# Attention heads placed between the query blocks of a fused two-block network, with the shifted turn beside the values and the last projection in column parts

## The chip, the cores and the metric

The kernel runs on one NeuronCore of one Trainium2 chip. The metric is the device time of one launch in microseconds, the median over three runs.

TensorE is PE in the profile (its weight loads PEld), ScalarE ACT, VectorE DVE, GpSimd POOL, SyncE SP (it only issues transfers). Each runs its own program in order; they meet at semaphores.

## What is computed

Sequence 256, model width 2048, all in float32. A first block (windowed attention, a recurrent unit, a layer of experts) and a state-space layer come first and stay as they are. The change is in the last layer, a dilated attention whose keys and values come from the unshifted input x of the layer:

```python
k, v = split(x @ kv_w, 2)                 # 3 groups x 8 heads x 128 each
h = x * (1 + scale) + shift               # scale, shift, gate: silu(c) @ ada_w + ada_b
q, z = split(h @ in_w, [3072])            # 3 x 8 x 128 query columns, 1024 for z
...
for g, (window, dilation) in enumerate(DIL_PATTERNS):
    o, lse = _dilated_window_attention(q[:, :, g], k_sh[:, :, g], v_sh[:, :, g],
                                       window, dilation, slopes[g])
...
o = einsum("blghe,blgh->blhe", o, softmax(lse over g)) * silu(z)
y = o @ out_w                             # 1024 x 2048
x = _layer_norm(ALPHA * x + (1.0 + gate) * y, ln_g, ln_b)
```

The three groups of a head share one softmax over all their scores, since the weights of the groups come from their log-sums.

## The kernel before

**Weights.** Every weight matrix is streamed in tiles of 128 x 1024 (512 KB) in the order of the table STREAM, four buffers deep. SyncE loads a tile into raw; ScalarE copies it to w_hi in TensorE's reduced format (L1119, "high part"; it waits until TensorE has done with the tile that had the buffer, four tiles before); VectorE subtracts to get the rest, w_lo (L1580, "low part"). TensorE forms each product as three matmuls: high with high, high with low, low with high. A tile's count goes through the semaphores raw_loaded, hi_done, lo_done and tile_used. FIRST_BODY[name] is the first group of four tiles of a matrix.

**Products.** The transposed input is held as xt_hi and xt_lo, 16 pieces of 128 channels x 256 tokens. In block_product two tiles give one block of 128 output channels (48 matmuls with 256 columns, L528 to L530), and banks 0 and 1 of PSUM alternate. In token_columns a tile gives 12 matmuls of 512 columns (L581 to L583), tokens on the partitions. For a new input, turn transposes X (L625), and ScalarE and VectorE make the 16 pieces (L1156, L1632, L1640).

**Order of the last layer.** k2 (24 blocks), v2 (3 groups of 16 tiles into banks 0 to 3; each is evicted at L1537 before the next), with the ada sums for this layer's scale and gate ahead of the third group; then the turn of the shifted input; q2 (24 blocks, evicted into q2T at L1544); z2 (16 tiles into banks 4 to 7, then Silu at L1551). Then the 8 heads, in a loop of two: GpSimd copies a head's three query pieces to q_st (L516), TensorE forms the scores (L1066, L1069), VectorE adds distances and finds the maxima (L2288 to L2303), ScalarE takes the exponentials (L1557, L1559), TensorE transposes them (L1077), ScalarE copies them out (L1562, L1564), TensorE multiplies with the values (L1082, L1086), and VectorE scales and gates (L2312) in zn. The eight outputs are transposed (L1104), copied to oT, split into high and low, and b_out (16 tiles, L600 to L604) accumulates all 2048 output columns in all 8 banks at once. Last, gate_rows spreads the gate over the partitions by matmuls with a diagonal (built by GpSimd, L490; matmuls L1034), and layer_norm runs over whole rows: product times gate (L2227), residual (L2230), sums and squares on ScalarE (L1517, L1521), root (L1160), and two operations a token half on VectorE (L2240, L2245), each half of the tokens then stored.

The text of each engine's program sets the order.

## Time and profile before

| | us |
|---|---|
| median of 3 runs | 3613.61 (3612.01 to 3614.05) |
| the profiled execution, its own time | 3612.69 |
| its span, first to last instruction | 3611.0 |
| TensorE busy in it | 3369.3 (93%) |
| granted TensorE clock, mean | 0.966 of 2.4 GHz |

The profile is of one execution; its times count from the first instruction, and v2 starts at 3120.6 us. Busy time of an engine says nothing of what it holds up: for that the waits and the chain of work are read. A granted clock (PEclk) of 1.00 is 2.4 GHz, 0.50 is 1.2 GHz.

### The profile page before, as it was taken

The numbers are of one execution on the slowest core, as the hardware profiler recorded it, in microseconds if no ns is written. First come the engines' busy times: TensorE is split into PE (matmuls) and PEld (weight loads), VectorE is DVE, ScalarE is ACT, GpSimd is POOL, SyncE is SP. The second block draws the span as 40 slices with busy tenths as digits, with TensorE's granted clock in tenths as the row PEclk, the third lists the DMA queues.
The fourth block names the chain that finished last, engine by engine and source line by source line (L and its number), as shares of the span: only waits on it lengthen the run. The fifth ranks groups of instructions, "written<-read, shape, count | busy, mean of one in ns | idle before, by whom it ended". The sixth has DMA issues, their size and how long they took to land.

```text
span 3611.0 us, 70869 instructions
## 1 busy us (share of the span) xinstructions
PE 3369.3 (93%) x24282; PEld 3043.7 (84%) x24282; DVE 2245.7 (62%) x3639; ACT 1636.7 (45%) x2226; POOL 679.6 (19%) x620
## 2 busy tenths in 40 slices
PE   7989999999999999999999889999997979999986
PEld 7878999999889988998778679987775859978965
DVE  6674476377777777777777743346554876545454
ACT  4654455433443345333445446653433444334443
POOL 1000049500110011000001148851113111100010
PEclk9999999999999999999999989999997989999998
DMA  6425545666886678666558725554443767755622
GB/s 189 147 82 164 162 143 162 181 203 201 261 262 197 203 240 266 213 203 187 164 159 272 236 83 182 182 164 147 135 141 107 264 211 233 243 177 151 184 78 93
DMA packets 181819, 656.59 MB, mean 182 GB/s; under 512 B 23040, under 2 KB 23184, under 8 KB 180576
## 3 DMA queue, kind: packets, MB, share of 16 engines
q1 hardware_dynamic: 149328, 545.82, 48.9%
q0 software_dynamic: 32400, 109.56, 9.7%
q8 instruction: 57, 0.93, 0.1%
q14 instruction: 34, 0.28, 0.0%
HBM read 653.18 MB, written 2.10 MB: 181 GB/s over the span
## 4 chain that ended last, share of the span: by engine, by line
PE 83%; DVE 5%; issue 4%; ACT 3%; PEld 2%; POOL 2%; DMA 0%; DVEq 0%; ACTq 0%; POOLq 0%; PEldq 0%; SPq 0%
PE PS L528 14%; PE PS L529 13%; PE PS L530 13%; PE PS L857 7%; PE PS L861 6%; PE PS L859 6%; PE PS L810 2%; PE PS L600 2%; PE PS L602 2%; PE PS L604 2%; PE PS L581 2%; PE PS L582 2%; PE PS L583 2%; POOL w_lo L429 2%; PE PS L1011 1%
## 5 line engine op out<-in xcount | busy, mean ns | idle before, releaser
L1119 ACT ACTIVATE w_hi<-raw 128x1024 fp32r<-128x1024 f32 x1032 | 1092.5, 1060 | 1657.0 <-PE PS L530 945.3
L1580 DVE TENSOR_TENSOR w_lo<-raw,w_hi 128x1024 fp32r<-128x1024 f32 x872 | 1070.9, 1230 | 898.2 <-ACT w_hi L1119 893.6
L528 PE MATMUL PS<-xt_hi,w_hi 128*128 128x256 f32 x4608 | 1326.3, 288 | 20.5 <-DVEq L2106 8.5
L529 PE MATMUL PS<-xt_lo,w_hi 128*128 128x256 f32 x4608 | 1309.6, 284 | 0.0
L530 PE MATMUL PS<-xt_hi,w_lo 128*128 128x256 f32 x4608 | 1308.8, 284 | 0.0
L528 PEld LDWEIGHTS PS<-xt_hi,w_hi 128*128 128x128 f32 x4608 | 890.0, 193 | 34.3 <-issue 25.6
L529 PEld LDWEIGHTS PS<-xt_lo,w_hi 128*128 128x128 f32 x4608 | 890.6, 193 | 0.0
L530 PEld LDWEIGHTS PS<-xt_hi,w_lo 128*128 128x128 f32 x4608 | 890.1, 193 | 0.0
L429 POOL TENSOR_TENSOR w_lo<-raw,w_hi 128x1024 fp32r<-128x1024 f32 x160 | 402.3, 2540 | 241.7 <-ACT w_hi L1119 241.3
L857 PE MATMUL PS<-w_hi,st_hi 128*128 128x512 f32 x1024 | 403.0, 394 | 0.2
L859 PE MATMUL PS<-w_hi,st_lo 128*128 128x512 f32 x1024 | 399.8, 390 | 0.0
L861 PE MATMUL PS<-w_lo,st_hi 128*128 128x512 f32 x1024 | 399.5, 390 | 0.0
L443 POOL DMA_DIRECT2D ada<-in_ada_w x240 | 128.9, 537 | 1230.1 <-DVE acc_down L1954 652.2
L857 PEld LDWEIGHTS PS<-w_hi,st_hi 128*128 128x128 f32 x1024 | 193.0, 188 | 40.3 <-ACT hid L1363 1.0
L861 PEld LDWEIGHTS PS<-w_lo,st_hi 128*128 128x128 f32 x1024 | 192.8, 188 | 40.3
L859 PEld LDWEIGHTS PS<-w_hi,st_lo 128*128 128x128 f32 x1024 | 193.0, 189 | 39.1
L581 PE MATMUL PS<-w_hi,xt_hi 128*128 128x512 f32 x352 | 140.8, 400 | 3.6 <-ACT v2n L1537 3.6
L600 PE MATMUL PS<-w_hi,st_hi 128*128 128x512 f32 x320 | 126.6, 396 | 14.8 <-DVE st_lo L1598 14.8
L582 PE MATMUL PS<-w_hi,xt_lo 128*128 128x512 f32 x352 | 138.9, 395 | 0.0
L583 PE MATMUL PS<-w_lo,xt_hi 128*128 128x512 f32 x352 | 138.8, 394 | 0.0
L1928 DVE TENSOR_TENSOR hot<-iota,slotsT 128x256 bf16<-128x256 bf16 (+1 forms) x256 | 113.4, 484 | 29.0 <-PEq L802 29.0
L602 PE MATMUL PS<-w_hi,st_lo 128*128 128x512 f32 x320 | 126.4, 395 | 0.0
(369 smaller groups left out, 3540.4 us busy)
## 6 DMA issues: line engine op xcount, KB each, us to landing
raw<-in_u_emb SPq DMA_DIRECT2D x256, 512.0 KB, 3.8
raw<-in_v_emb SPq DMA_DIRECT2D x256, 512.0 KB, 4.3
ada<-in_ada_w POOLq DMA_DIRECT2D x240, 256.0 KB, 3.7
raw<-in_xbc SPq DMA_DIRECT2D x96, 512.0 KB, 3.9
raw<-in_z SPq DMA_DIRECT2D x80, 512.0 KB, 3.6
raw<-in_q SPq DMA_DIRECT2D x64, 512.0 KB, 3.5
raw<-in_a_out SPq DMA_DIRECT2D x64, 512.0 KB, 4.8
raw<-in_k SPq DMA_DIRECT2D x48, 512.0 KB, 4.2
```

The costliest lines, as they stand in the source:

```text
L429: pool.tensor_tensor(w_lo[:, u, :], raw[:, u, :], w_hi[:, u, :].bitcast(F32), ALU.subtract)\
L528: pe.matmul(o, w_h, x_h, start=start, stop=False, skip_group_check=True)
L529: pe.matmul(o, w_h, x_l, start=False, stop=False, skip_group_check=True)
L530: return pe.matmul(o, w_l, x_h, start=False, stop=stop, skip_group_check=True)
L581: pe.matmul(o, xt_hi[:, k, t], w_hi[:, u, c:c + 512], start=k == 0, stop=False)
L582: pe.matmul(o, xt_lo[:, k, t], w_hi[:, u, c:c + 512], start=False, stop=False)
L583: last = pe.matmul(o, xt_hi[:, k, t], w_lo[:, u, c:c + 512], start=False, stop=k == KC - 1)
L857: pe.matmul(o, st(st_hi, st2_hi, u)[:, t], w_hi[:, u, c], start=start, stop=False, skip_group_check=True)
L859: pe.matmul(o, st(st_lo, st2_lo, u)[:, t], w_hi[:, u, c], start=False, stop=False, skip_group_check=True)
L861: last = pe.matmul(o, st(st_hi, st2_hi, u)[:, t], w_lo[:, u, c], start=False, stop=stop, skip_group_check=True)
L1119: act.activation(w_hi[:, u, :], raw[:, u, :], ACT.Copy).then_inc(hi_done, 1)
L1580: dve.tensor_tensor(w_lo[:, u, :], raw[:, u, :], w_hi[:, u, :].bitcast(F32), ALU.subtract)\
```

## The change

z2 is streamed ahead of q2. The values are made in 6 groups of 8 tiles that alternate between banks 0, 1 and 2, 3. The ada sums and the 16 transposes of the shifted input stand between tiles of the values, and the shifted pieces go to buffers of their own (xt2_hi, xt2_lo, q2T is gone). The columns of q2 are stored head by head, so that blocks 3h to 3h+2 give the queries of head h, which ScalarE evicts straight into q_st; the steps of head h stand between the blocks of head h+1, those of the last head between tiles of b_out. The outputs of each head are transposed and split into o_hi and o_lo at once. b_out is taken in four parts of 512 columns (two banks each), in the order OUT_TILES; the gate row is spread between its tiles, and VectorE adds a part and takes its statistics with BN_STATS while later parts run. The norm is finished by half rows, which are stored in four transfers. The last layer's steps on TensorE, ScalarE and VectorE are written out without loops, except k2 and z2 on the latter two.

```diff
-    ("xbc", 24), ("z", 16), ("a_out", 16), ("k2", 12), ("v2", 12), ("q2", 12), ("z2", 4), ("b_out", 4),
+    ("xbc", 24), ("z", 16), ("a_out", 16), ("k2", 12), ("v2", 12), ("z2", 4), ("q2", 12), ("b_out", 4),
...
+OUT_TILES = [(part, pair) for part in (0, 1) for pair in range(3)] + [(0, 3), (1, 3)] \
+    + [(part, pair) for part in (2, 3) for pair in range(4)]
...
-            pool.wait_ge(act_free, 2 + ACT_BLOCKS["q2"] + 24)
-            with pool.Fori(0, DH) as h:
-                pool.wait_ge(sem("head_scored"), h + 1)
-                pool.tensor_copy(q_st[:, :, :],
-                                 q2T[:, :, :].rearrange("p (g h) s -> p g h s", g=DG)[:, :, ds(h, 1), :]
-                                 .rearrange("p g o s -> p g (o s)")).then_inc(sem("q_staged"), 1)
-            pool.wait_ge(sem("q_staged"), DH)
-            norm_operands(1)
-            norm_rows(1)
+            pool.wait_ge(tile_used, 4 * FIRST_BODY["b_out"])
+            for part in range(2):
+                pool.tensor_tensor(last_diag[:, part, :].rearrange("p (c k) -> p c k", k=P),
+                                   ident.unsqueeze(1).to_broadcast([P, KC, P]),
+                                   gate_part[:, 1, part, :].bitcast(F32).unsqueeze(2).to_broadcast([P, KC, P]),
+                                   ALU.mult).then_inc(sem("gates_diagonal"), 1)
+            pool.wait_ge(sem("head_product"), DH)
+            for r in range(2):
+                pool.dma_start(last_rows[:, r, :], a["rows"][3 + r].partition_broadcast(P))\
+                    .then_inc(sem("last_rows_loaded"), 16)
...
-            with pe.Fori(0, DG - 1) as g:
-                pe.wait_ge(sem("v2_out"), g + 1)
-                token_columns(16 * g, FIRST_BODY["v2"], 0, 1)
-            pe.wait_ge(sem("mod_done"), 10)
-            ada_sum("kv2", 3, ada_acc_k)
-            pe.wait_ge(sem("v2_out"), DG)
-            token_columns(16 * (DG - 1), FIRST_BODY["v2"], 0, 1)
-            pe.wait_ge(sem("mod_done"), 11)
-            pe.wait_ge(sem("v2_out"), DG + 1)
-            turn(4)
-            turned_blocks("q2", act_free, ACT_BLOCKS["q2"], 4)
-            token_columns(0, FIRST_BODY["z2"], 4, 1)
+            def turn_shifted(c):
+                if c >= 4:
+                    pe.wait_ge(sem("xt2_low"), c - 3)
+                for tt in range(TT):
+                    last = pe.transpose(PS[:, 4 + c % 4, tt * P:tt * P + P], X[:, tt, c * P:c * P + P], ident)
+                last.then_inc(sem("xt2_turned"), 1)
+            for g in range(2 * DG):
+                if g >= 2:
+                    pe.wait_ge(sem("v2_out"), g - 1)
+                def between(i):
+                    t = 8 * g + i
+                    if t == 21:
+                        pe.wait_ge(sem("mod_done"), 10)
+                        ada_sum("kv2", 3, ada_acc_k)
+                    if 26 <= t < 26 + KC:
+                        if t == 26:
+                            pe.wait_ge(sem("mod_done"), 11)
+                        turn_shifted(t - 26)
+                token_columns(8 * g, FIRST_BODY["v2"], 2 * (g % 2), 2, after=between)
+            pe.wait_ge(sem("xt2_low"), KC)
+            shifted_source = (xt2_hi, xt2_lo)
+            token_columns(0, FIRST_BODY["z2"], 4, 1, source=shifted_source)
+            pe.wait_ge(sem("v2_out"), 2 * DG)
             pe.wait_ge(sem("z2_out"), 1)
...
-                pe.wait_ge(sem("q_staged"), h + 1)
-                pe.wait_ge(sem("dist_added"), h + 1)
+                pe.wait_ge(act_free, 2 + ACT_BLOCKS["q2"] + 3 * h + 3)
+                if h:
+                    pe.wait_ge(sem("dist_added"), h)
+                    pe.wait_ge(sem("pT2_done"), h)
...
+            def head_probs(h):
                 pe.wait_ge(sem("head_exp"), h + 1)
+                if h:
...
+            def head_values(h):
                 pe.wait_ge(sem("pT2_done"), h + 1)
-                pe.wait_ge(sem("head_out"), h + 1)
+                if h:
+                    pe.wait_ge(sem("o_low"), h)
...
+            def head_turn(h):
+                pe.wait_ge(sem("head_out"), h + 1)
                 for tt in range(TT):
...
+                    last = pe.transpose(PS[:, 7, S + tt * P:S + tt * P + P], zn[:, tt, h * P:h * P + P], ident)
+                last.then_inc(sem("o_turned"), 1)
+            for i in range(24):
+                h, k = i // 3, i % 3
+                pe.wait_ge(act_free, ACT_BLOCKS["q2"] + i + 1)
+                block_product("q2", i // 2, i % 2, PS[:, i % 2, 0:S], shifted_source)
+                if h and k == 0:
+                    head_probs(h - 1)
+                if h and k == 1:
+                    head_values(h - 1)
+                if k == 2:
+                    if h:
+                        head_turn(h - 1)
+                    head_scores(h)
...
+            def out_tile(i):
+                part, pair = OUT_TILES[i]
+                pe.wait_ge(lo_done, 4 * FIRST_BODY["b_out"] + i + 1)
+                pe.wait_ge(sem("o_low"), 2 * pair + 2)
+                for k in range(2):
+                    chunk = 2 * pair + k
+                    for tt in range(TT):
+                        o, t, c = PS[:, 2 * part + tt, :], slice(tt * P, tt * P + P), slice(k * 512, k * 512 + 512)
+                        pe.matmul(o, o_hi[:, chunk, t], w_hi[:, i % 4, c], start=chunk == 0, stop=False,
+                                  skip_group_check=True)
+                        pe.matmul(o, o_lo[:, chunk, t], w_hi[:, i % 4, c], start=False, stop=False,
+                                  skip_group_check=True)
+                        last = pe.matmul(o, o_hi[:, chunk, t], w_lo[:, i % 4, c], start=False, stop=chunk == DH - 1,
+                                         skip_group_check=True)
+                last.then_inc(tile_used, 1)
...
+            pe.wait_ge(act_free, 2 + ACT_BLOCKS["q2"] + 24)
+            for i in range(16):
+                if i == 3:
+                    pe.wait_ge(sem("dist_added"), DH)
+                if i == 12:
+                    pe.wait_ge(sem("last_gates_out"), 2)
+                out_tile(i)
+                if i == 1:
+                    head_probs(DH - 1)
+                if i == 3:
+                    head_values(DH - 1)
+                if i == 4:
+                    head_turn(DH - 1)
+                if i == 7:
+                    last_gates(0)
+                if i == 9:
+                    last_gates(2)
...
+            def values_out(g):
+                act.wait_ge(tile_used, 4 * f + 8 * g + 8)
+                bank = 2 * (g % 2)
+                act.activation(v2n[:, :, g * 512:(g + 1) * 512], PS[:, bank:bank + 2, :], ACT.Copy)\
+                    .then_inc(sem("v2_out"), 1)
...
+            for t in range(48):
+                high(f + 1 + t // 4, t % 4)
+                if t % 8 == 7:
+                    values_out(t // 8)
+                if 27 <= t < 27 + KC:
+                    c = t - 27
+                    if c == 0:
+                        act.wait_ge(sem("mod_done"), 12)
+                    act.wait_ge(sem("xt2_turned"), c + 1)
+                    act.activation(xt2_hi[:, c, :], PS[:, 4 + c % 4, 0:S], ACT.Identity,
+                                   scale=mod[:, 64 + c:65 + c], bias=mod[:, 48 + c:49 + c]).then_inc(sem("xt2_high"), 1)
...
+            def head_query(i):
+                act.wait_ge(tile_used, 4 * f + 2 * i + 2)
+                if i % 3 == 0 and i:
+                    act.wait_ge(sem("head_scored"), i // 3)
+                act.activation(q_st[:, i % 3, :], PS[:, i % 2, 0:S], ACT.Copy, scale=float(P) ** -0.5)\
+                    .then_inc(act_free, 1)
...
+            for i in range(24):
+                h, k = i // 3, i % 3
+                if h > 1 and k == 0:
+                    head_high(h - 2)
+                if h and k == 1:
+                    head_probs(h - 1)
+                high(f + 1 + i // 2, 2 * (i % 2))
+                if h and k == 0:
+                    head_exp(h - 1)
+                high(f + 1 + i // 2, 2 * (i % 2) + 1)
+                head_query(i)
+            f = FIRST_BODY["b_out"]
...
+            head_high(DH - 2)
+            for i in range(12):
+                high(f + 1 + i // 4, i % 4)
+                if i == 0:
+                    head_exp(DH - 1)
+                if i == 1:
+                    head_probs(DH - 1)
...
+            for t in range(16, 48):
+                low(f + t // 4, t % 4)
+                if t == 19:
+                    mod_add(60, 12, 0, 9).then_inc(sem("mod_done"), 1)
+                    dve.wait_ge(sem("mod_done"), 11)
+                    dve.tensor_scalar(mod[:, 64:80], mod[:, 64:80], 1.0, None, ALU.add).then_inc(sem("mod_done"), 1)
+                    dve.wait_ge(sem("mod_done"), 12)
+                if 27 <= t < 27 + KC:
+                    dve.wait_ge(sem("xt2_high"), t - 27 + 1)
+                    shifted(t - 27)
+                    shifted_low(t - 27)
...
+            for i in range(24):
+                h, k = i // 3, i % 3
+                if h > 1 and k == 0:
+                    head_low(h - 2)
+                if h and k == 0:
+                    head_maxima(h - 1)
+                if h and k == 2:
+                    head_outputs(h - 1)
+                low(f + i // 2, 2 * (i % 2))
+                low(f + i // 2, 2 * (i % 2) + 1)
+            f = FIRST_BODY["b_out"]
...
+            def add_part(part):
+                c = slice(part * 512, part * 512 + 512)
+                dve.wait_ge(tile_used, 4 * f + (7, 8, 12, 16)[part])
+                if part == 0:
+                    dve.wait_ge(sem("last_gates_out"), 2)
+                for tt in range(TT):
+                    link.post(dve.tensor_tensor(last_product[:, tt, :], PS[:, 2 * part + tt, :], gate_row[:, c], ALU.mult))
+                for tt in range(TT):
+                    link.wait(1)
+                    link.post(dve.scalar_tensor_tensor(X[:, tt, c], X[:, tt, c], ALPHA, last_product[:, tt, :],
+                                                       ALU.mult, ALU.add))
+                for tt in range(TT):
+                    link.wait(1)
+                    link.post(dve.bn_stats(bn[:, tt, part, :], X[:, tt, c]))
+            head_low(DH - 2)
+            head_maxima(DH - 1)
+            for i in range(12):
+                low(f + 1 + i // 4, i % 4)
+                if i == 3:
+                    head_outputs(DH - 1)
+                if i == 5:
+                    head_low(DH - 1)
+            for part in range(4):
+                add_part(part)
+            link.wait()
+            for tt in range(TT):
+                last = dve.bn_aggr(moments[:, tt, :], bn[:, tt, :, :].rearrange("p a b -> p (a b)"))
+                if tt == 0:
+                    link.post(last)
+            last.then_inc(sem("ln_moments"), 1)
+            dve.wait_ge(sem("ln_moments"), 1)
...
+            centred(0, 0)
+            centred(0, 1)
+            dve.wait_ge(sem("ln_root"), 2)
+            link(dve.reciprocal(stat[:, 8:10], stat[:, 6:8]))
+            finished(0, 0)
+            finished(0, 1)
+            centred(1, 0)
+            centred(1, 1)
+            link.wait()
+            finished(1, 0)
+            finished(1, 1)
```

What is not shown is the same work at other banks and buffers: head_exp, head_high (a copy into o_hi) and head_probs on ScalarE, head_maxima and head_outputs on VectorE, last_gates, and shifted and shifted_low, which make a piece as L1632 and L1640 did.

On TensorE, in the head stage: before, what follows one another for the last two heads (sc are the scores and probabilities, pT the turned ones, cc the identity).

```order
L1069 MATMUL PS<-k2T,q_st 128x256
L1077 MATMUL PS<-cc,sc 128x128 x9
L1082 MATMUL PS<-v2n,pT 128x128 x3
L1086 MATMUL PS<-v2n,pT 128x128 x6
L1077 MATMUL PS<-cc,sc 128x128 x9
L1082 MATMUL PS<-v2n,pT 128x128 x3
L1086 MATMUL PS<-v2n,pT 128x128 x6
L1104 MATMUL PS<-cc,zn 128x128 x16
```

Now, at the end of block 3h+2 (its last matmuls first, zn the outputs of head h-1, then the scores of head h) and the start of the next block.

```order
L551 MATMUL PS<-xt_hi,w_lo 128x256
L1140 MATMUL PS<-cc,zn 128x128 x2
L1104 MATMUL PS<-k2T,q_st 128x128
L1106 MATMUL PS<-k2T,q_st 128x256
L1104 MATMUL PS<-k2T,q_st 128x128
L1106 MATMUL PS<-k2T,q_st 128x256
L1104 MATMUL PS<-k2T,q_st 128x128
L1106 MATMUL PS<-k2T,q_st 128x256
L549 MATMUL PS<-xt_hi,w_hi 128x256
L550 MATMUL PS<-xt_lo,w_hi 128x256
L551 MATMUL PS<-xt_hi,w_lo 128x256
```

The matmuls of a head no longer follow one another; those of the query blocks stand between all its steps, and scores stand directly behind the block that makes the last of their queries.

On ScalarE, one round of a head before (a table load, the exponentials, the copies of the turned probabilities).

```order
L1557 ACT_TABLE_LOAD
L1557 ACTIVATE sc,sm<-sc,sm 128x384
L1559 ACTIVATE sc,sm<-sc,sm 128x768
L1561 REGISTER_ALU
L1562 ACTIVATE pT<-PS 128x1024
L1564 ACTIVATE pT<-PS 128x128
```

Now, from the start of a head's first block to the end of its second.

```order
L1677 ACTIVATE o_hi<-PS 128x256
L1211 ACTIVATE w_hi<-raw 128x1024
L1660 ACTIVATE sc,sm<-sc,sm 128x384
L1662 ACTIVATE sc,sm<-sc,sm 128x768
L1211 ACTIVATE w_hi<-raw 128x1024
L1654 ACTIVATE q_st<-PS 128x256
L1670 ACTIVATE pT<-PS 128x1024
L1672 ACTIVATE pT<-PS 128x128
L1211 ACTIVATE w_hi<-raw 128x1024 x2
L1654 ACTIVATE q_st<-PS 128x256
L1211 ACTIVATE w_hi<-raw 128x1024 x2
L1654 ACTIVATE q_st<-PS 128x256
```

The same steps stand among high parts (L1211), and each query eviction (L1654) stands behind the two high parts of its turn.

On VectorE, before: the norm, whole rows at a time, behind the last projection.

```order
L2222 COPY Y<-PS 128x2048
L2227 TENSOR_TENSOR Y<-Y,PS 128x2048 x2
L2230 SCALAR_TENSOR_TENSOR X<-X,Y 128x2048 x2
L2235 TENSOR_SCALAR stat<-stat 128x1
L2240 SCALAR_TENSOR_TENSOR Y<-X,stat,rows 128x2048
L2235 TENSOR_SCALAR stat<-stat 128x1
L2240 SCALAR_TENSOR_TENSOR Y<-X,stat,rows 128x2048
L2243 RECIPROCAL stat<-stat 128x2
L2245 SCALAR_TENSOR_TENSOR X<-Y,stat,rows 128x2048 x2
```

Now, from four low parts of b_out on, around head 7's output (o_lo), to the first column part.

```order
L1722 TENSOR_TENSOR w_lo<-raw,w_hi 128x1024 x4
L2468 RECIPROCAL sm<-sm 128x2
L2472 SCALAR_TENSOR_TENSOR zn<-PS,sm,zn 128x128 x2
L1722 TENSOR_TENSOR w_lo<-raw,w_hi 128x1024 x2
L2481 TENSOR_TENSOR o_lo<-PS,o_hi 128x256
L1722 TENSOR_TENSOR w_lo<-raw,w_hi 128x1024 x6
L2504 TENSOR_TENSOR last_product<-PS,gate_row 128x512 x2
L2507 SCALAR_TENSOR_TENSOR X<-X,last_product 128x512 x2
L2511 BN_STATS bn<-X 128x6 x2
```

The low half of head 7's output stands behind two more low parts, and the parts of the norm stand behind the last six.

## Rows read from the trace of the kernel before

**Rows 1.** Page: span; costliest groups (count, busy us, mean ns of one, idle before).
```profile
span 3611.0 us, 70869 instructions
...
PE 3369.3 (93%) x24282; PEld 3043.7 (84%) x24282; DVE 2245.7 (62%) x3639; ACT 1636.7 (45%) x2226; POOL 679.6 (19%) x620
...
L1580 DVE TENSOR_TENSOR w_lo<-raw,w_hi 128x1024 fp32r<-128x1024 f32 x872 | 1070.9, 1230 | 898.2 <-ACT w_hi L1119 893.6
```

**Rows 2.** Windows by stage: length, busy us and instructions by engine, PEclk, DMA.
```profile
79.00:150.00 71.00, 71.00 (x322) 59.50 (x321) 39.84 (x34) 50.31 (x89) 0.00 (x0) 1.00 0.49 149
3120.60:3276.50 155.90, 147.13 (x633) 119.62 (x632) 75.96 (x83) 64.16 (x70) 5.37 (x10) 0.93 0.61 185
3276.50:3417.40 140.90, 140.84 (x1153) 140.87 (x1154) 63.19 (x60) 56.29 (x71) 0.00 (x0) 0.98 0.57 171
3417.40:3460.90 43.50, 43.50 (x192) 35.66 (x190) 19.61 (x16) 17.24 (x17) 0.00 (x0) 1.00 0.62 191
3460.90:3533.60 72.70, 49.38 (x329) 44.09 (x329) 37.08 (x99) 34.56 (x59) 13.82 (x10) 0.93 0.05 17
3533.60:3579.00 45.40, 45.38 (x192) 37.12 (x192) 16.92 (x19) 14.56 (x18) 0.00 (x0) 0.96 0.29 93
3579.00:3611.00 32.00, 3.16 (x9) 2.01 (x8) 20.88 (x12) 11.65 (x11) 1.11 (x2) 0.55 0.33 131
```

**Rows 3.** Waits of TensorE from 3120 us on: us, times, longest us.
```profile
PE PS L1082 <- ACT pT L1564: 10.8, 8, 1.4
```

**Rows 4.** Windows: two around a pause between value groups, shifted turn, head loop.
```profile
3214.30:3217.40 3.10, 2.69 (x25) 2.61 (x23) 1.23 (x1) 2.88 (x3) 0.00 (x0) 0.94 0.63 190
3217.40:3220.40 3.00, 2.95 (x7) 2.37 (x8) 0.00 (x0) 0.00 (x1) 0.00 (x0) 0.50 0.61 175
3262.70:3276.50 13.80, 8.64 (x32) 5.74 (x32) 9.81 (x22) 10.66 (x19) 0.00 (x0) 0.58 0.27 79
3477.00:3523.00 46.00, 35.30 (x266) 31.87 (x263) 30.74 (x85) 23.88 (x46) 11.68 (x8) 1.00 0.00 1
```

**Rows 5.** Windows in one head: scores, nine transposes, values.
```profile
3480.92:3482.89 1.97, 1.97 (x14) 1.77 (x13) 0.61 (x2) 1.08 (x4) 0.00 (x0) 1.00 0.00 0
3482.89:3483.87 0.98, 0.98 (x10) 0.90 (x8) 0.64 (x3) 0.00 (x0) 0.65 (x1) 1.00 0.00 0
3485.41:3487.52 2.11, 2.11 (x19) 2.11 (x19) 1.54 (x4) 1.72 (x3) 0.00 (x0) 1.00 0.00 0
```

**Rows 6.** Timeline of ScalarE at one q2 block: start us, us, what.
```profile
3284.93 1.06 ACT L1119 ACTIVATE w_hi<-raw 128x1024 fp32r<-128x1024 f32 x1 [1.81 <-PE PS L530]
3285.89 0.37 ACT L1544 ACTIVATE q2T<-PS 128x256 f32 x1
```

**Rows 7.** Timeline of VectorE, then ScalarE, in one head.
```profile
3483.23 0.86 DVE L2288 SCALAR_TENSOR_TENSOR sc<-cd,PS 128x128 f32<-128x128 f32 x3 [1.30 <-PE PS L1069]
...
3486.75 0.17 DVE L2303 TENSOR_SCALAR sm<-sm 128x2 f32<-128x2 f32 x1
...
3485.29 1.28 ACT L1557 ACT_TABLE_LOAD   x1
...
3488.39 0.19 ACT L1559 ACTIVATION_READ_ACCUMULATOR sc<-sc,sm 128x1 f32 x1
```

**Rows 8.** Timeline of ScalarE behind z2.
```profile
3463.38 1.94 ACT L1551 ACTIVATE zn<-PS 128x1024 f32<-128x1024 f32 x2
```

**Rows 9.** Timeline of GpSimd, then VectorE, ahead of a_out.
```profile
2757.60 7.42 POOL L490 TENSOR_TENSOR gate_diag<-cc,gate_part 128x2048 fp32r<-128x2048 f32 x2 [3.44 <-ACT rg L1160]
...
2761.07 5.02 DVE L2187 SCALAR_TENSOR_TENSOR xbc<-xbc,pc,rg 128x256 f32<-128x256 f32 x4
```

**Rows 10.** Timeline of the last norm: VectorE, and the last transfer's issue.
```profile
3584.78 4.49 DVE L2227 TENSOR_TENSOR Y<-Y,PS 128x2048 f32<-128x2048 f32 x2 [3.40 <-PE PS L1034]
...
3601.86 4.61 DVE L2245 SCALAR_TENSOR_TENSOR X<-Y,stat,rows 128x2048 f32<-128x2048 f32 x2
...
3606.50 0.35 SPq L407 DMA_DIRECT2D out<-X  x1
```

266 lines of the change are left out of this document (139 added, 127 removed).

## The prediction

> **What bounds the kernel now.** I read the page first: of a span of 3611.0 us TensorE is busy 93% [rows 1]. So only stretches where it stands still, or runs below full clock, can give time. The change touches only what comes after the k2 blocks, so I cut the end into stages by windows. The reader should see that the three weight stages (values v2, queries q2, gate z2) are full or nearly so, while the head stage keeps TensorE busy 49.38 of 72.7 us and the last norm 3.16 of 32.0 us [rows 2]. Then the waits: TensorE waits 8 times up to 1.4 us for the turned probabilities [rows 3]. Last the clock: behind the 3.1 us between two groups of values, in which it ran only the small matmuls of the ada sums, TensorE ran 3.0 us at 0.50; through the head stage, with 35.30 busy of 46.0 us and a pause of 1.4 us in each head, it kept 1.00 [rows 4].
>
> From these come unit prices at full clock. A tile of 12 matmuls of 512 columns: 43.5/16 = 2.72 us. A block of 48 matmuls of 256 columns: 140.9 x 0.98/24 = 5.75 us [rows 2]. One head: scores 1.97, nine transposes 0.98 (0.109 each), values 2.11 us [rows 5]. One high part on ScalarE 1.06, one query eviction 0.37, together 1.33 from the block's end [rows 6]; one low part on VectorE 1.23 [rows 1].
>
> **Values, with the shifted turn between tiles.** Before: 155.9 us [rows 2]. Now 48 tiles x 2.72 = 130.6; the cold start as before, 1.7 (some 3.4 us at half clock); the ada sums, which stood in a pause before (2.69 us busy there [rows 4]), now on the path, 2.7; 32 transposes x 0.109 = 3.5. Sum 138.5. The values go to two pairs of banks in turn, so an eviction (ACT L1537, half as much at a time, about 1 us) has a whole group of eight tiles, 21.8 us, to hide in. The shifted operand is made one of its 16 pieces a tile. Before, ScalarE and VectorE were busy 10.66 and 9.81 us in the 13.8 us of the turn [rows 4], while they made at least ten pieces, so a piece costs either engine about 1 us at most; with the weights' 1.06 and 1.23 that is 2.2 us of a tile of 2.72 + 0.22, and both keep up. If that cover failed it would cost at most those 13.8 us again. **Gain 17.4.** z2 moves ahead of q2 at 43.5 us each way: nothing.
>
> **Queries and heads, one stage now.** Before 140.9 + 72.7 = 213.6 us [rows 2]. TensorE still waits for the Silu ahead of the first q2 block (table load and two halves, ending at 3465.32, so 4.4 us [rows 8]), and then runs cold, 2.6 (between one and two cold stretches, 1.7 to 3.4). Its work: 24 x 5.75 = 138.1; scores 8 x 1.97 = 15.8; transposes 7 x 0.98 = 6.9; values 7 x 2.11 = 14.8; turned outputs 7 x 0.22 = 1.5. The pauses between heads go under the blocks, but two waits come:
>
> (a) The scores of head h need query 3h+2, and that block is the last thing TensorE did. ScalarE starts on the eviction only behind a high part that waits for the same block: 1.33 us [rows 6], plus some 0.2 for the matmul's own drain and the signal; the two output transposes fill 0.2 of it. 8 x 1.4 = 11.3. Queued behind it are the scores and every block after; nothing covers it.
>
> (b) The exponentials. Count from the block's end T: scores run T+1.6 to T+3.6, VectorE's maxima take 3.69 (3483.23 to 3486.92), the exponentials 1.66 (to 3488.58) [rows 7], so they end near T+9.4. ScalarE cannot start them before its high part for the half block, ready at T+7.7, which changes nothing. TensorE comes to the transposes at T+3.6+5.75 = T+9.35. Even within 0.2 us: 7 x 0.2 = 1.4, and for head 0 the Exp table load of 1.28 [rows 7] on top: 2.5 in all, between 0 and 5.
>
> Sum 4.4 + 2.6 + 138.1 + 15.8 + 6.9 + 14.8 + 1.5 + 11.3 + 2.5 = 197.9. **Gain 15.7.** The period of a head should be 17.25 + 1.97 + 0.98 + 2.11 + 0.2 + 1.4 + 0.2 = 24.1 us.
>
> **Last projection.** Before 45.4. Now 16 tiles 43.5; head 7's transposes, values and turn 0.98 + 2.11 + 0.22 = 3.3; the gate row's 8 matmuls, moved here from the tail, 8 x 0.227 = 1.8. Two waits again:
>
> (c) GpSimd builds last_diag just as head 7's maxima are due. Its two instructions of this form took 7.42 us, and beside them VectorE's four operations of 256 elements with two SBUF inputs took 5.02 us, where 2048 elements take 2.30 [rows 10]: one was held until GpSimd had ended [rows 9]. A low part has two SBUF inputs, so the one at T+1.1 waits about 2.5 us, and the maxima, exponentials and transposes of head 7 behind it: TensorE waits 1.9 at its third step here, 0 if the low part comes first, 5 if both instructions hold it. The Trainium skill ("SBUF — State Buffer", SBUF: two separate sides) says the same: GpSimd and a two-input VectorE instruction exclude each other for a whole instruction; the trace agrees with its 5.02 us.
>
> (d) Tile 6 needs o_lo of head 7, and VectorE's queue has low part 9 ahead of it, which needs TensorE's tile 5: high part 1.06, low part 1.23, o_lo 0.4, signals 0.3: 3.0 us, with nothing beside it. A pause of this size was followed by 3 us at 0.50 before [rows 4]; half a chance of 1.7, so 0.8.
>
> Sum 43.5 + 3.3 + 1.8 + 1.9 + 3.0 + 0.8 = 54.3. **Loss 8.9.**
>
> **Last norm.** Before 32.0. The copy of the product, the two passes of sums on ScalarE and most adding leave the path. VectorE's price is 2.25 us per 2048 elements times a PSUM row and 2.30 per 2048 otherwise [rows 10], so about 0.66 for 512 and 1.18 for 1024. Parts 0 to 2 are queued behind low part 15, so they start 8.4 us before the last matmul ends; 18 operations x 0.66 = 11.9 overrun it by 3.5, and part 3 adds 6 x 0.66 = 4.0. BN_STATS is not in this trace; I take 0.66, since it reads as many elements as its neighbours. At twice that the eight of them add 5.3, all behind one another on the path; at half they save 2.6. Moments and mean 0.6, then eight half-row operations 8 x 1.18 = 9.4 and the reciprocal 0.3, which the root hides under. The end is a transfer: 4.5 us from issue to the span's end for 1 MB before [rows 10]; for half of it I take 3.7 (2.3 to 4.5). Sum 3.5 + 4.0 + 0.6 + 9.7 + 3.7 = 21.5. **Gain 10.5.** The Sqrt table load (1.28) stood on the path; now it waits for nothing and goes ahead of ScalarE's last wait. The Trainium skill ("ScalarE: Activation LUTs", What ACT_TABLE_LOAD costs) gives about 2.66 us for a switch, its drain included; the trace shows 1.28 and the next work 0.02 us behind. By the page head 0 would lose 1.4 more and the sum would be 3580.5.
>
> **Sum:** 17.4 + 15.7 - 8.9 + 10.5 = 34.7 us less. Against the profiled execution (span 3611.0, its own time 3612.69) that is 3576.3 and 3578.0; that execution is 0.9 below the median of the runs, 3613.61, so 3578.9, say 3579.
>
> **Rivals.** (1) *More waits, 3588 to 3605.* The exponentials come late in every head (VectorE's low parts before the maxima; 1 us x 8), each 1.4 us wait brings a cold stretch (8 x 1.7 = 13.6), or BN_STATS and the lock cost their upper ends. For it: (b) has no margin. Against: eight pauses of 1.4 us left the clock at 1.00 [rows 4], and here they are 24 us apart. 10%.
> (2) *The waits are hidden, 3560 to 3568.* Without (a), (b) and (d) 17 us more. Against (a) speaks the queue itself; only (b) and (d) can shrink. 6%.
> (3) *Slower.* TensorE falls to 1.2 GHz in the joined stage and stays there while heads and blocks alternate. Its 177 us of work at full clock would cost 177 more at half; it decides from one fifth of it, 35 us, where the gain is gone. By the trace the granted clock fell at pauses of 3 us and more, and the stage has one such at its start. 4%.
> (4) *No change.* The stages lose their loops, so TensorE runs some 2,300 matmuls, two instructions each, as straight code; if each came 7.5 ns late on average, 35 us would be gone. Against it: 71.0 us of such code early in the kernel had TensorE busy 71.00 [rows 2]. 2%.
>
> **How the numbers follow.** My forecast, 3568 to 3588, has 78%. The range 3567 to 3592 leaves out the far side of (1), (2), (3) and (4). Faster by over 0.2% (7 us, about what a measurement tells from none) has 94%, within 0.2% 2%, slower 4%.
>
> **What would show it.** Values stage some 138 us with no pause over 0.5; eight pauses of about 1.4 us ahead of L1104, released by the query eviction (ScalarE), 24 us apart; a pause of about 3 us at the seventh tile of b_out, released by o_lo; GpSimd's last_diag with a long low part beside it; 21 to 22 us from the last matmul to the end. Wrong it would be made by long pauses released by weights (w_lo) in the q2 stage, or a granted clock below 0.97 there.

## The result, and the profile after

The changed kernel takes 3575.86 us (median of 4 runs, 3574.52 to 3576.61) beside 3613.25 us before (3612.01 to 3614.05); the ratio is 0.9898, with a 95% interval of 0.9885 to 0.991. That is 37.4 us less; 34.7 were forecast, and 3575.86 lies within the range and within the likeliest case. The profiled execution took 3576.61 us. Of the kernels below, one execution of diag_later (11465.58 us) and one of mended_parts_behind (5725.64 us, the profiled one) stand far above all others of their kernel and are left out of the medians.

Windows of the changed kernel at its own stage borders: values, z2, queries with heads, last projection, behind the last matmul (columns as in [rows 2]).

```profile
core 0 of [0], span 3574.9 us
...
3118.70:3258.10 139.40, 139.40 (x633) 114.81 (x634) 80.64 (x95) 61.63 (x68) 5.36 (x10) 0.99 0.62 198
3258.10:3301.60 43.50, 43.50 (x192) 35.68 (x191) 19.61 (x16) 17.88 (x17) 0.00 (x0) 1.00 0.60 194
3301.60:3498.80 197.20, 181.13 (x1453) 177.56 (x1452) 93.32 (x139) 83.14 (x126) 3.44 (x1) 0.98 0.40 131
3498.80:3555.30 56.50, 52.35 (x230) 42.39 (x228) 29.22 (x42) 18.80 (x22) 5.83 (x4) 0.94 0.34 121
3555.30:3574.90 19.60, 0.00 (x0) 0.00 (x0) 16.33 (x22) 0.29 (x1) 0.00 (x0) 0.62 0.26 107
```

| stage | before, us | forecast | after |
|---|---|---|---|
| values | 155.9 | 138.5 | 139.4 |
| z2 | 43.5 | 43.5 | 43.5 |
| queries and heads | 213.6 | 197.9 | 197.2 |
| last projection | 45.4 | 54.3 | 56.5 |
| behind it | 32.0 | 21.5 | 19.6 |
| sum | 490.4 | 455.7 | 456.2 |

The stages give 34.2 us. The other 1.9 us between the two profiled executions lie ahead of v2 (3118.7 instead of 3120.6), nearly all in the first 370 us, which the change doesn't touch; the profiled executions of the kernels here (but for that of 5725.64 us), whose work is the same up to TensorE's long pause at some 2952 us, reach it between 2950.76 and 2954.18 us, 3.4 us apart. So a single execution can't carry a claim under about 3 us unless it is read from a fixed point inside the trace, and below I do that.

Where TensorE waits from 3110 us on: of eight waits for pT [rows 3] there is nothing left, and four kinds are new (us, times, longest us).

```profile
PE PS L1104 <- ACT q_st L1654: 10.3, 8, 1.5
PE PS L549 <- issue: 4.5, 1, 4.5
PE PS L1165 <- DVE o_lo L2481: 2.9, 1, 2.9
PE PS L1117 <- ACT sc L1662: 2.5, 2, 1.3
```

Sum: 20.2 us. In the 436.6 us from v2 to the last matmul these, and the clock, are all that stands between TensorE and full work. (For the second kind the view names no releaser; the Silu ends just ahead of it, and experiment 6 shows that it is the wait for the Silu.) Before, the longest waits beside those for pT were these; all eleven kinds make 34.6 us.

```profile
PE PS L1066 <- POOL q_st L516: 5.5, 1, 5.5
PE PS L581 <- ACT v2n L1537: 3.6, 2, 3.1
PE PS L625 <- ACT v2n L1537: 3.1, 1, 3.1
PE PS L600 <- DVE st_lo L1598: 3.0, 1, 3.0
```

The clock counts nearly as much as the waiting. Between v2 and the last matmul the trace of before has seven stretches of 3.41 us and one of 17.07 us at 0.50, with 39.6 us of TensorE's work in them, half of which, 19.8 us, are lost; the trace after has one of 3.41 us and two of 6.83, with 14.1 us of work, 7.1 lost. So of the 34.1 us that the two traces differ by from the pause at 2952 us on, 14.4 are waiting, 12.7 clock, 6.7 come behind the last matmul (26.4 before, 19.7 after), and 0.3 are neither.

The chain of work that ended last shows the first kind (start us, us, what):

```profile
3375.22 1.06 ACT w_hi L1211
3376.27 0.28 ACT q_st L1654
3376.60 0.49 PE PS L1104 x2
```

The block's last matmul is at 3375.13; the high part stands ahead of the eviction on ScalarE, and only then may the scores start (TensorE waits 1.26 us): 1.3 us on the path for 0.3 us of need. The third kind, in the same view:

```profile
3520.24 1.06 ACT w_hi L1211
...
3521.33 1.23 DVE w_lo L1722
3522.56 0.34 DVE o_lo L2481
...
3523.04 0.77 PE PS L1165
```

Again a part that nobody needs yet (the w_lo of tile 9, while TensorE stands at tile 6) runs first. What the pause costs beside its own 2.9 us is in the windows ahead of it, in it and behind it:

```profile
3516.50:3520.10 3.60, 3.60 (x17) 2.61 (x15) 1.23 (x1) 1.33 (x2) 0.00 (x0) 1.00 0.98 395
3520.10:3523.04 2.94, 0.05 (x2) 0.03 (x1) 1.56 (x2) 1.06 (x1) 0.00 (x0) 0.88 1.01 418
3523.04:3529.10 6.06, 6.06 (x14) 4.76 (x15) 0.00 (x0) 0.51 (x1) 0.00 (x0) 0.50 0.41 142
```

6.06 us of matmuls at 0.50 (1.2 GHz) are 3.0 us lost, more than the wait itself. Last, the timelines of GpSimd and of VectorE at the end of the last query block:

```profile
3495.36 8.16 POOL L535 TENSOR_TENSOR last_diag<-cc,gate_part 128x2048 fp32r<-128x2048 f32 x2 [338.01 <-PE PS L551]
```

```profile
3493.59 1.23 DVE L1722 TENSOR_TENSOR w_lo<-raw,w_hi 128x1024 fp32r<-128x1024 f32 x1 [2.95 <-ACT w_hi L1211]
3496.46 3.59 DVE L1722 TENSOR_TENSOR w_lo<-raw,w_hi 128x1024 fp32r<-128x1024 f32 x1 [1.65 <-ACT w_hi L1211]
```

The same operation takes 1.23 us alone and 3.59 us beside GpSimd's. GpSimd's 8.16 us are two instructions, and the low part ends 1.08 us behind the end of the first (3498.97).

### The profile page after: what moved, and what is told of

It reads as the page before. It is cut to its first block, busy times and chain, and to the rows that moved or that the text cites. A ratio compares the mean times of both kernels' runs of the same rounds, so it can differ in the third digit from the quotient of the medians.

```text
span 3574.9 us, 70325 instructions
## 1 busy us (share of the span) xinstructions
PE 3357.0 (94%) x24282; PEld 3035.0 (85%) x24282; DVE 2251.5 (63%) x3663; ACT 1619.2 (45%) x2215; POOL 673.6 (19%) x612
## 4 chain that ended last, share of the span: by engine, by line
PE 83%; DVE 6%; issue 3%; ACT 3%; PEld 2%; POOL 2%; DMA 1%; DVEq 0%; SPq 0%; POOLq 0%; PEldq 0%; ACTq 0%
PE PS L549 14%; PE PS L550 13%; PE PS L551 13%; PE PS L879 7%; PE PS L881 6%; PE PS L883 6%; PE PS L832 2%; PE PS L603 2%; PE PS L605 2%; PE PS L604 2%; POOL w_lo L448 2%; PE PS L622 2%; PE PS L626 2%; PE PS L624 2%; ACT w_hi L1211 1%
## 5 line engine op out<-in xcount | busy, mean ns | idle before, releaser
L1211 ACT ACTIVATE w_hi<-raw 128x1024 fp32r<-128x1024 f32 x1032 | 1092.4, 1060 | 1682.0 <-PE PS L551 973.8
L879 PE MATMUL PS<-w_hi,st_hi 128*128 128x512 f32 x1024 | 403.0, 394 | 0.2
L881 PE MATMUL PS<-w_hi,st_lo 128*128 128x512 f32 x1024 | 399.7, 390 | 0.0
L1808 DVE TENSOR_SCALAR cbuf<-PS,pc 128x256 f32<-128x256 f32 x48 | 23.2, 484 | 159.6 <-PE PS L551 81.2
L622 PE MATMUL PS<-w_hi,st_hi 128*128 128x512 f32 x256 | 100.9, 394 | 11.8 <-DVE st_lo L1740 11.8
```

The source lines that it names most:

```text
L879: pe.matmul(o, st(st_hi, st2_hi, u)[:, t], w_hi[:, u, c], start=start, stop=False, skip_group_check=True)
L881: pe.matmul(o, st(st_lo, st2_lo, u)[:, t], w_hi[:, u, c], start=False, stop=False, skip_group_check=True)
L1211: act.activation(w_hi[:, u, :], raw[:, u, :], ACT.Copy).then_inc(hi_done, 1)
```

## The experiments

Experiments 1 to 7 each undo or move one thing in the changed kernel; 8 and 9 join several edits, and 10 edits the kernel before. Times are medians; the kernel before was timed beside each batch at 3612.1 to 3612.9 us. A difference of medians can be wrong by some 2 us between batches, so I read each also inside its trace, from TensorE's 20.6 us pause at 2952 us, which all have, to its last matmul and to the end of the span. In the changed kernel these are 603.6 and 623.3 us.

| kernel | us | ratio to before, 95% | to last matmul | to end |
|---|---|---|---|---|
| before | 3613.25 | | 631.0 | 657.4 |
| changed | 3575.86 | 0.9898 (0.9885 to 0.991) | 603.6 | 623.3 |
| turn_apart | 3592.36 | 0.9944 (0.9928 to 0.9959) | 618.8 | 638.4 |
| parts_late | 3584.92 | 0.9925 (0.9909 to 0.994) | 601.8 | 630.1 |
| query_first | 3570.25 | 0.988 (0.9865 to 0.9896) | 596.7 | 616.4 |
| low_sooner | 3570.64 | 0.9885 (0.9869 to 0.99) | 597.6 | 617.2 |
| diag_later | 3574.42 | 0.9896 (0.9878 to 0.9914) | 600.8 | 620.5 |
| silu_later | 3569.90 | 0.9882 (0.9867 to 0.9897) | 595.0 | 614.6 |
| head_bare | 3665.28 | 1.0148 (1.0132 to 1.0163) | 691.7 | 711.4 |
| all_mended | 3553.13 | 0.9835 (0.9822 to 0.9849) | 581.9 | 599.4 |
| mended_parts_behind | 3554.53 | 0.9841 (0.9828 to 0.9855) | | |
| before_unrolled | 3609.94 | 0.9991 (0.9982 to 1.0001) | 629.1 | 655.4 |

**1. The turn beside the values, undone (turn_apart).**

```diff
-                    if 26 <= t < 26 + KC:
-                        if t == 26:
-                            pe.wait_ge(sem("mod_done"), 11)
-                        turn_shifted(t - 26)
 
                 token_columns(8 * g, FIRST_BODY["v2"], 2 * (g % 2), 2, after=between)
+            pe.wait_ge(sem("mod_done"), 11)
+            for c in range(KC):
+                turn_shifted(c)
```

ScalarE's and VectorE's pieces move behind the last value tile in the same way.

> The changed kernel with one part undone: the 16 transposes of the shifted input, and the pieces that ScalarE and VectorE make of them, stand behind the last tile of the values and not between tiles. If the turn was hidden by the tiles (my theory), this brings back most of the 13.8 us that it took before, less the eviction of 3.1 us that now goes to other banks, and a cold start of z2 behind it: 11 to 14 us slower than the changed kernel, about 3588. A rival says that the pause was the eviction and the wait for scale and shift, and the turn itself is little more than its 3.5 us of transposes: then 0 to 2 us slower.

Measured: 16.5 us slower, more than I expected (11 to 14). TensorE's waits up to z2:

```profile
PE PS L1073 <- DVE xt_lo L2418: 6.6, 12, 2.8
PE PS L603 <- DVE xt_lo L2418: 3.2, 1, 3.2
```

and the window over the turn:

```profile
3252.00:3274.00 22.00, 12.20 (x46) 6.90 (x45) 16.61 (x34) 11.59 (x19) 0.00 (x0) 0.69 0.23 73
```

The waits are 9.8 us. Behind the pause of 2.81 us for the first free bank, and while the transposes come with pauses of 0.3 us between them, the clock is at 0.50 for 17.07 us, into z2's tiles. z2 ends 16.3 us later, counted from the pause at 2952 us: 9.8 waiting, and 5.6 half clock in the 11.2 us that TensorE works within that stretch, so about a third is clock, not waiting. The rival falls: a turn on its own costs much more than its transposes.

That 16.3 is close to the 16.5 us that the values stage gained is a coincidence. Before, the turn took 13.8 us [rows 4] and the transposes between tiles now take 4.3, so the turn gave 9.5 in this stage, and 2.7 us of half clock in the first q2 block besides. The other 6.8 come from the borders between value groups, 3.6 waiting (L581 above) and two stretches of 3.41 us at 0.50; the changed kernel has neither. No run undoes the alternation of banks, so this part is read from the rows alone. turn_apart pays more than these 12.2 for its turn, in part because z2 waits until all sixteen pieces are there (3.2 us), where the first q2 block of before took them as they came (0.4).

**2. The norm's parts, undone (parts_late).**

```diff
-                dve.wait_ge(tile_used, 4 * f + (7, 8, 12, 16)[part])
+                dve.wait_ge(tile_used, 4 * f + 16)
```

> The changed kernel with one part undone: VectorE adds all four column parts only when the last tile of the projection is done. The column parts are all there still. My theory says that what the tail gained by them is the work that runs ahead of the last matmul, 8.55 us in the profile of the changed kernel: 8.6 us slower, about 3584.5, and the stretch from the last matmul to the end 28.2 us in place of 19.6. A rival says that the gain comes from the statistics of BN_STATS, the moved gate row and the half-row stores, and parts running beside matmuls slow each other: then under 4 us slower.

Measured: 9.1 us slower. The end of the span comes 28.2 us behind the last matmul, which ends at 3554.31, instead of 19.7: 8.6 us, as expected, and the rival falls. What VectorE does of the additions ahead of TensorE's end is gained in full.

**3. The query's eviction first (query_first).**

```diff
-                high(f + 1 + i // 2, 2 * (i % 2) + 1)
                 head_query(i)
+                high(f + 1 + i // 2, 2 * (i % 2) + 1)
```

> The changed kernel with ScalarE's eviction of a query block ahead of the high part that waits for the same block. My theory says that 1.06 of the 1.26 us that TensorE waits ahead of each head's scores is that high part. Eight times that is 8.5 us, but the exponentials have no slack against the next transposes and come up to 0.35 us late in seven heads: 6 us faster than the changed kernel, about 3570 (3567 to 3571), the wait ahead of the scores 0.1 to 0.3 us. A rival says that the wait is the drain of the last matmul and the signals: no change.

Measured: 5.6 us faster, 6.9 to the last matmul. Its waits:

```profile
PE PS L1117 <- ACT sc L1662: 3.5, 2, 2.2
PE PS L1165 <- DVE o_lo L2481: 2.9, 1, 2.9
PE PS L1104 <- ACT q_st L1654: 2.3, 8, 0.5
```

L1104 falls from 10.3 to 2.3 us, so most of that wait was the high part, and the rival falls. 1.0 us comes back at L1117: TensorE reaches the last head sooner, and the exponentials behind the held low part don't. That pause is now 2.24 us long, and the clock is at 0.50 for 3.41 us behind it, 1.7 us lost. High parts were not late for it: no wait for w_hi or w_lo appears.

**4. The last o_lo one low part sooner (low_sooner).**

```diff
-                if i == 5:
+                if i == 4:
                     head_low(DH - 1)
```

> Edit to the changed kernel: VectorE takes the scaled subtraction of the last head (o_lo, head 7) behind its third low part of the last projection's tile stretch instead of behind its fourth, that is one low part (1.23 us and its wait for a tile) sooner. In the changed kernel TensorE waits 2.89 us for this o_lo ahead of column tile 6, and the clock stands at 0.5 from 2.2 us behind the wait's start for 6.83 us, of which 6.1 us are matmuls (3.05 us of cost). My theory: the wait is set by the place of o_lo in VectorE's order and the cold stretch by the wait. The wait falls to about 0.3 us, the clock stays at 1.00, and the kernel comes to 3575.9 - 2.6 - 3.0 = 3570.3 us (3569.5 to 3571.5). Rival A: the wait is set by the head's own chain (exponentials, outputs), not by VectorE's order; then nothing moves, 3575.9. Rival B: the wait goes but another one, for the low part that is now later, takes its place: 3573 to 3576, and TensorE shows a wait on w_lo behind tile 5.

Measured: 5.2 us faster, 6.0 to the last matmul. The wait is gone from the view, and so is the half clock:

```profile
3518.00:3528.00 10.00, 10.00 (x45) 7.99 (x44) 4.82 (x5) 3.98 (x5) 0.00 (x0) 1.00 0.87 339
```

2.9 us of wait and 3.0 us of clock make 5.9; both rivals fall.

**5. last_diag behind the last exponentials (diag_later).**

```diff
-            pool.wait_ge(tile_used, 4 * FIRST_BODY["b_out"])
+            pool.wait_ge(sem("head_exp"), DH)
```

> Edit to the changed kernel: GpSimd builds last_diag (two TENSOR_TENSOR, 8.16 us together) behind the last head's exponentials instead of behind the last tile of the queries, so not beside VectorE's low part at 3496.46, which took 3.59 us there and 1.23 us elsewhere. My theory: the low part takes 1.23 us again, the wait of 1.23 us of the last head's scores multiplication goes, and 3575.9 - 1.2 = 3574.7 us (3574.0 to 3575.5); the effect is small and its interval may touch 1. Rival: GpSimd's work collides with VectorE wherever it lies in this stretch, so another VectorE operation (o_lo or the low parts of tiles 4 to 7) takes 2 us more, the wait ahead of tile 6 grows from 2.9 to about 5 us, and the kernel is 1 to 2 us slower (3577 to 3578).

Measured: 1.4 us faster, within what the interval can tell; so the trace has to show it. VectorE's timeline in the old place, and beside GpSimd's work, now from 3504.82:

```profile
3496.79 1.23 DVE L1722 TENSOR_TENSOR w_lo<-raw,w_hi 128x1024 fp32r<-128x1024 f32 x1 [1.65 <-ACT w_hi L1211]
...
3505.97 3.54 DVE L1722 TENSOR_TENSOR w_lo<-raw,w_hi 128x1024 fp32r<-128x1024 f32 x1 [1.50 <-ACT w_hi L1211]
3509.93 5.26 DVE L1722 TENSOR_TENSOR w_lo<-raw,w_hi 128x1024 fp32r<-128x1024 f32 x2 [0.42 <-ACT w_hi L1211]
```

and in the waits of TensorE only head 0's is left of L1117:

```profile
PE PS L1117 <- ACT sc L1662: 1.3, 1, 1.3
```

The first low part is back at 1.23 us. The collision has moved and not gone: the first half of the rival is right, since one low part beside GpSimd's work takes 3.54 us, and two more 5.26 where two take 2.4. The other half is wrong: TensorE still waits 2.9 us ahead of tile 6 and for no low part, so nobody on the path is held. To the last matmul the trace is 2.8 us shorter, but only 1.2 of that is this wait; 1.3 is the clock behind (d), at 0.50 for 3.41 us in this execution and for 6.83 in that of the changed kernel, which the edit has no part in as far as the trace shows. The Trainium skill ("SBUF — State Buffer", SBUF: two separate sides) says that of such a pair of operations the one that starts first has the SBUF ports that the two engines share for its whole instruction. The trace agrees in who waits: in the changed kernel GpSimd began at 3495.36, VectorE at 3496.46, and VectorE lost 2.36 us.

**6. The wait for the Silu ahead of the first scores (silu_later).**

```diff
             pe.wait_ge(sem("v2_out"), 2 * DG)
-            pe.wait_ge(sem("z2_out"), 1)
...
                     if h:
                         head_turn(h - 1)
+                    else:
+                        pe.wait_ge(sem("z2_out"), 1)
                     head_scores(h)
```

> Edit to the changed kernel: TensorE's wait for the z2 gates' Silu (z2_out) stands ahead of the first head's scores instead of ahead of the first query tile. In the changed kernel TensorE pauses 4.50 us there and then runs 4.6 us of matmuls at clock 0.5 (2.3 us of cost). My theory: the query blocks don't need the Silu, whose 1.9 us and the evictions ahead of it then lie beside two query tiles; 3575.9 - 4.5 - 2.3 = 3569.1 us (3568.3 to 3570.5). Rival: the pause only moves, because the first query block's high part on ScalarE stands behind the Silu in any case and TensorE waits for that instead (tile slots of the same banks, or q_st of head 0): then 2 to 4.5 us of it stay and the cold stretch too, 3573 to 3576.

Measured: 6.0 us faster. The window over the border of z2 and q2:

```profile
3290.00:3320.00 30.00, 30.00 (x198) 27.66 (x197) 12.90 (x11) 15.32 (x16) 0.00 (x0) 1.00 0.57 185
```

TensorE is busy 30.00 of 30.00 us at 1.00, and the rival falls. (To the last matmul the trace is 8.6 us shorter, 1.6 of which are the clock behind (d) again.) I left this pause in the forecast as it had been before ("TensorE still waits for the Silu"); none of the first three query blocks uses what it waits for.

**7. The heads bare (head_bare).** The old order was not tried in the new kernel (all queries at once are 24 KB a partition, beside two copies of the input); this takes the cover away instead.

```diff
-                if h and k == 0:
-                    head_probs(h - 1)
-                if h and k == 1:
-                    head_values(h - 1)
                 if k == 2:
-                    if h:
-                        head_turn(h - 1)
                     head_scores(h)
+                    head_probs(h)
+                    head_values(h)
+                    head_turn(h)
```

TensorE's part of it; the last head's steps leave the tiles of b_out, and ScalarE's and VectorE's steps move in the same way.

> Edit to the changed kernel: each head's chain runs bare, ahead of the next query block, on all three engines: scores, maxima, exponentials, transposes, copies of the weights, values, outputs, the head's transposes, and only then the next block. No query block lies beside a head any more; the computation is the same. From the rows of head 3 in the changed kernel TensorE then waits for each head for the additions and maxima (3.7 us) and both exponentials (1.6 us), for the copies of the weights (1.3 us) and for the outputs (0.6 us), 7.2 us, with some 1.2 us of passing on between engines, so 8.4 us; the wait ahead of the scores (1.3 us each) stays. My theory: the query blocks hide exactly this chain, and pauses of 5 us also bring a stretch at clock 0.5 for every head (1.7 to 3.4 us of cost): 8 x (8.4 + 2.5) = 87, less the last head's wait, cold stretch and exponentials in the last projection (8 us), so 3655 us (3638 to 3672). Rival A: the clock doesn't fall, 3575.9 + 67 - 8 = 3635 us. Rival B: what the blocks hide is less, because ScalarE's and VectorE's own tile work, moved behind the head, was in the way before: under 3625 us.

Measured: 3665.28 us, 89.4 more. The waits from 3300 us on:

```profile
PE PS L1117 <- ACT sc L1653: 44.5, 8, 6.4
PE PS L1104 <- ACT q_st L1645: 11.8, 8, 1.5
PE PS L1126 <- ACT pT L1663: 10.3, 8, 1.3
PE PS L1140 <- DVE zn L2457: 6.3, 8, 0.9
PE PS L549 <- issue: 4.5, 1, 4.5
```

and a window of 100 us in the stage:

```profile
3400.00:3500.00 100.00, 74.56 (x498) 70.77 (x497) 32.84 (x54) 27.39 (x43) 0.00 (x0) 0.83 0.24 79
```

Each head waits 5.4 + 1.3 + 0.8 = 7.5 us. Its period, from the first head's wait at L1104 to the last's (3324.50 to 3578.08), is 36.2 us; in the changed kernel the same seven periods (3325.63 to 3495.49) take 24.3 each: 12.0 more, of which 7.5 are waiting and 4.2 the clock, which stood at 0.50 for 6.8 to 13.7 us in every head. I had put the waits a little too high (8.4) and the clock too low (2.5). Rivals A and B fall. That is what the query blocks hide in this kernel. It is not what the change gained over the old order, which already put the scores of the next head beside the maxima and exponentials of one: there the two stages of queries and heads gained 16.4 us.

**8. All five places (all_mended).** The edits 3 to 6, and the first three parts between the last low parts:

```diff
-                if part == 0:
-                    dve.wait_ge(sem("last_gates_out"), 2)
+                if part in (0, 2):
+                    dve.wait_ge(sem("last_gates_out"), part // 2 + 1)
...
+                if i in (9, 10, 11):
+                    add_part(i - 9)
-            for part in range(4):
-                add_part(part)
+            add_part(3)
```

> The changed kernel with five places altered at once: the query's eviction ahead of the second high part on ScalarE (alone: 5.6 us less), the last o_lo one low part sooner (forecast 5.6 less), last_diag behind the last exponentials (1.2), the z2 wait ahead of the first scores (6.8), and the final addition's parts 0 to 2 between VectorE's last low parts so that they start when their tiles are done (3.6 from the tail, which is 19.6 us now). My theory is that these are separate places in series on TensorE's path: 5.6 + 5.6 + 1.2 + 6.8 + 3.6 = 22.8 less, 3553.1 us (3550.5 to 3556). Rival: the parts of the addition between the low parts hold back the low parts, and TensorE waits for them at tiles 14 and 15 (VectorE needs 1.28 us for each addition row beside 1.23 for a low part every 2.8 us), which gives the 3.6 back and may cool the clock: 3556 to 3562.

Measured: 3553.13 us (3552.03 to 3554.72), 22.7 less than the changed kernel and 59.0 less than before in the same batch. Waits of TensorE from 3110 us on:

```profile
PE PS L1103 <- ACT q_st L1655: 2.3, 8, 0.6
PE PS L1116 <- ACT sc L1663: 1.3, 1, 1.3
```

Windows over queries with heads, last projection, and behind the last matmul:

```profile
3302.00:3492.00 190.00, 186.30 (x1485) 181.11 (x1484) 97.98 (x151) 85.96 (x132) 0.15 (x1) 1.00 0.43 142
3492.00:3535.60 43.60, 43.54 (x205) 35.79 (x204) 30.30 (x34) 16.07 (x17) 9.11 (x4) 1.00 0.39 145
3535.60:3553.00 17.40, 0.00 (x0) 0.00 (x0) 14.13 (x18) 0.30 (x1) 0.00 (x0) 0.57 0.30 121
```

In this part the clock is 1.00 up to the last matmul, and the rival falls: no wait for a low part appears. To the last matmul it saves 21.8 us, and the pieces, as read above, give 6.8 (Silu and clock) + 5.9 (o_lo and clock) + 1.2 (lock) + 8.0 (eviction) = 21.9: they are in series and add up. The four single edits' own differences at this point sum to 24.4; three of their traces also had the shorter stretch behind (d), and query_first paid at the last head.

**9. One of the five taken back (mended_parts_behind).** As all_mended, with the four parts behind the last low part again.

> The kernel with five places altered, with one of them taken back: the final addition's four parts again stand behind VectorE's last low part, as in the changed kernel. In the kernel with all five the additions end 3.7 us behind the last matmul (one part, six operations of 0.6 us), in the changed kernel 5.8 us behind it. My theory: that is all there is to it, 2.1 us, since TensorE waited for no low part in either, so 3555.2 us (3554.2 to 3556.5), not the 3.6 us that I forecast for this piece. Rival: the low parts, freed of the additions between them, run further ahead and the last tiles end sooner, so the difference is near 0 or negative: 3551.5 to 3553.5.

Measured: 3554.53 us, ratio 0.9841 (0.9828 to 0.9855), 1.4 us over all_mended. The intervals overlap, and its trace is of the 5725.64 us execution (mean clock 0.66) and can't be set beside the others, so this run decides neither for my 2.1 us nor for the rival. What stands for the 2.1 are the last windows of the two traces, 19.6 less 17.4. My 3.6 us for this piece were too much: it can give back only what parts 0 to 2 overran the last matmul by, and in the changed kernel that was 2.3 us (the last of their nine pairs ends at 3557.58, TensorE at 3555.28), since an operation takes 0.60 us.

**10. The kernel before, its loops written out (before_unrolled).** TensorE's loops over value groups, query blocks and heads in the kernel before become straight code; nothing else. The loop over query blocks, not shown, is replaced in the same way.

```diff
-            with pe.Fori(0, DG - 1) as g:
+            for g in range(DG - 1):
...
-            with pe.Fori(0, DH // 2 - 1) as j:
+            for j in range(DH // 2 - 1):
```

> The kernel before, with TensorE's loops over the values' groups, the q2 blocks and the heads written out, in the same order of work. My theory has the whole gain in pauses and order, none in the code's form: within 2 us of the kernel before, 3613. A rival says that loops cost TensorE something at each turn which the changed kernel saves, or that straight code comes late: 3 us or more to either side.

Measured: 3609.94 us beside 3612.92, 3.0 us less, on the border between my 2 and the rival's 3; the ratio's interval, 0.9982 to 1.0001, just holds 1. From the pause at 2952 us to TensorE's wait ahead of the heads it takes 507.3 us in both kernels: as straight code 24 query blocks cost and save nothing. In the head stage, the waits from 3110 us on are

```profile
PE PS L1088 <- ACT pT L1570: 10.3, 8, 1.3
```

which is 0.09 us less in each of six heads (1.28 for 1.37 us) than [rows 3] has, and the windows from the seventh wait for pT to the start of b_out show the clock, before

```profile
3517.07:3533.62 16.55, 9.35 (x61) 8.48 (x62) 4.63 (x14) 6.61 (x11) 0.62 (x1) 0.90 0.00 0
```

and with straight code

```profile
3515.21:3530.06 14.85, 7.72 (x62) 6.89 (x62) 4.56 (x14) 6.61 (x11) 0.63 (x1) 0.99 0.00 0
```

So the head stage is 2.3 us shorter (70.4 for 72.7): 0.6 in the loop, and 1.7 behind it, where the execution of before ran one stretch of 3.41 us at half clock more. Whether straight code brings that second part isn't shown. The Trainium skill ("Runtime: NRT & Kernel Launch", Instruction fetch mechanics) says that a taken branch whose target is not among the instructions already loaded costs a fetch, one reason to prefer straight code; no such cost shows at the eleven turns of the query loop here. So by the medians TensorE's straight code may be worth 3 of the 37.4 us; the trace shows 0.6 of it in the loop, and the rest stays open.

## Why the prediction was right, point by point

The waits that it named are there, each where it put it. That the sum is so near (455.7 and 456.2 us) is in part luck: the stages are off by +0.9, 0, -0.7, +2.2 and -1.9.

**Values** (forecast 138.5, measured 139.4; turn_apart shows the turn's part of the gain, the 6.8 us of the group borders are read from rows). No wait, as said. One term was small by 0.9: a tile with a piece of the turn took 2.99 us, not 2.72 + 0.22; a pair of transposes between tiles costs 0.27, 16 x 0.05 = 0.8.

**Queries and heads** (197.9, 197.2). The wait for the Silu was 4.5 us (4.4), the half clock behind it 4.6 us of matmuls, 2.3 (2.6). But the Silu wait was taken over as if it had to stay, and silu_later shows that it need not. (a) is shown by query_first: eight waits, 10.3 us (11.3). (b) was too careful: only head 0 waits, 1.27 us, which is its table load; heads 1 to 6 wait for nothing (I had 1.4 for them, and 1.4 and 1.28 make 2.7, not the 2.5 of the sum).

```profile
3333.40 1.28 ACT L1660 ACT_TABLE_LOAD   x1
3334.69 0.61 ACT L1660 ACTIVATE sc<-sc,sm 128x384 f32<-128x384 f32 x1
```

The Trainium skill ("ScalarE: Activation LUTs", What ACT_TABLE_LOAD costs) gives 1.28 us for the load, which the trace has too, and 2.66 with a drain. By 2.66, head 0 would have waited about 2.7, an estimate; the work starts 0.01 us behind the load, and the measurement decides for 1.28. In the other heads the cover of 5.75 us of block was just enough. The period of heads 1 to 7 is 24.03 us (24.1). head_bare shows that it is the blocks that hide the chain. These terms are 2.4 us under the forecast and the stage only 0.7, since TensorE's own work took 178.8 us at full clock (181.13 busy less 2.3) for the 177.1 of the sum.

**Last projection** (54.3, 56.5). (c) The low part lost 2.36 us (2.5 forecast), and TensorE 1.23 (1.9): shown by diag_later. (d) 2.89 us (3.0) is shown by low_sooner. **The step that was mis-sized is the clock behind (d)**: "half a chance of 1.7, so 0.8" measured 3.0 in the profiled execution. I had halved a cost that the row showed in full after a stretch of the same size [rows 4]. Behind the same pause, 2.89 us long, turn_apart, query_first, parts_late, diag_later and silu_later had a stretch of 3.41 us at 0.50, and the changed kernel's profiled execution one of 6.83: so 1.4 to 3.0 us of lost work (where the stretch began inside the pause, less of it fell on matmuls), never nothing in these six. Some 0.7 us of the stage are in no term.

Behind it stands a reading of the clock that was too kind. I wrote that it fell at pauses of 3 us and more and that eight pauses of 1.4 us left it at 1.00. In the same trace it also fell behind a pause of 2.35 us (3470.22, then 0.50 from 3473.05), and the window of [rows 4] ends ahead of the eighth short pause. The last ones, 1.28, 0.84 and 1.28 us in 6.9 us, are followed by half clock:

```profile
3517.07:3524.25 7.18, 3.78 (x29) 3.35 (x30) 3.45 (x10) 4.01 (x8) 0.62 (x1) 1.00 0.00 0
3524.25:3527.66 3.41, 3.41 (x18) 3.37 (x16) 0.00 (x0) 0.00 (x0) 0.00 (x0) 0.50 0.00 0
```

**Last norm** (21.5, 19.6; parts_late shows 8.6 of the 12.4 us gained, the rest is not taken apart). VectorE begins 8.55 us before the last matmul ends (8.4). BATCH_NORM_STATS2, which I had to guess at 0.66 us, takes 0.60, like its neighbours, and all 24 operations 14.5 us (15.9): 5.9 us of them lie behind the last matmul (7.5). The last transfer ends 3.1 us behind VectorE's last half row (3.7), and the Sqrt table load isn't on the path, as said: it runs at 3545.57, and its work starts at 3561.62.

**The rivals.** (1) waits in every head: fell, heads 1 to 6 have no late exponentials, and eight pauses of 1.26 to 1.48 us left the clock at 1.00. (3) half clock in the joined stage: fell (0.98); even in head_bare, with three waits a head, one of them 5.4 us, the clock came back in every head, and the mean is 0.83. (4) straight code: fell (before_unrolled is no slower, and TensorE is busy 139.40 of 139.40 us in the values). (2), waits hidden, was no outcome of this kernel, but its 3560 to 3568 were available: all_mended is at 3553.13, below it, because it also takes the Silu's wait, the lock's and 2 us of the tail, and because hiding a wait gives the clock back too.

What is not settled: why the gain of the medians is 3 us over that of the stages (37.4 and 34.2). 1.9 of it lie ahead of v2 in the two traces, and 1.3 come from the places of the two profiled executions among the others of their kernels (0.6 under the median before, 0.8 above it after). Execution-to-execution differences ahead of the change are of that size (up to 3.4 us), but three or four executions of a kernel don't show that they explain it.

## What to carry to other kernels

When steps are woven into a stream of tiles, look at each queue at the point where the stream hands over, and put what TensorE waits for ahead of what is only prefetch; here four such edits of one to three lines were worth 22 us, more than half of what the large change gave. Price a pause of TensorE at its length, and from 2.2 us on, the shortest single pause that lowered the clock here, add 1.4 to 3 us for the half clock behind it. A lone pause of 1.5 us costs only its length, but eight of them were the largest single piece (8.0 us). Check for each wait at a stage border which operation behind it really needs it.

## What the runs showed of the hardware

- Eight pauses of 1.26 to 1.48 us, 24 us apart, never lowered the granted clock. One of 2.24 us did (query_first, at the last head, 3.41 us at 0.50), as did those of 2.35 and 2.48 us in the last layer of before, and all of 2.8 us and more in the changed part. The Trainium skill ("TensorE: Matmul & The Clock Gate", What's actually happening) says that the number of slow matmuls differs from run to run of the same kernel. The six kernels with the same 2.89 us pause, one execution of each, fit that: 3.41 us at 0.50 in five, 6.83 in one.
- In head_bare pauses of 5.44, 1.28 and 0.77 us within 14 us brought 6.83 us at 0.50 in three heads, 13.65 in four, and 10.24 in the last; the single pause of 4.50 us at the Silu brought 6.83, of which 2.3 lay inside the pause. Three short ones, 1.28, 0.84 and 1.28 us in 6.9 us, brought 3.41 us at 0.50 in before, and nearly the same three brought none in before_unrolled.
- GpSimd's tensor_tensor of 128 x 2048 (3.6 us alone) and VectorE's of 128 x 1024 with two SBUF inputs (1.23 us alone) hold each other up: side by side VectorE's took 3.54 us (diag_later) and 3.59 (changed kernel), and GpSimd's second one 4.59.
- Between tiles a pair of float32 transposes cost TensorE 0.27 us, where a pair out of a row of nine cost 0.22.
